# The gated product of the expert pairs on GpSimd, in two operations, in place of VectorE

## What is computed

```python
# top-4 of 32 experts per token; rows sorted by expert, cut into blocks
gu = xe @ w_gu[e] + b_gu[e]                       # 1024 -> 2048
gate = jnp.minimum(gu[..., 0::2], 7.0)
up = jnp.clip(gu[..., 1::2], -7.0, 7.0)
act = (up + 1.0) * (gate * jax.nn.sigmoid(gate * 1.702))
y = act @ w_dn[e] + b_dn[e]                       # 1024 -> 1024
out = zeros.at[row_tok].add(y * row_gate)
```

## Time and profile before

| | |
|---|---|
| median of 3 runs | 1425.97 us |
| profiled execution, own time | 1428.16 us |
| its span | 1426.5 us |
| PE matmul busy | 1331.1 us, 93% |
| PE weight load busy | 1058.9 us, 74% |
| VectorE (DVE) busy | 1276.3 us, 89% |
| ScalarE (ACT) busy | 1026.1 us, 72% |
| GpSimd (POOL) busy | 439.6 us, 31% |
| moved by DMA | 472.83 MB, mean 331 GB/s |
| splits on VectorE, L1004 | 409 of 2283 ns mean |
| copies on ScalarE, L645 | 409 of 1921 ns mean |

### The profile page before, as it was taken

The page is one execution under the profiler, slowest core; times in us unless marked ns, Lnnn a source line. Parts: engine busy times, 40 slices in busy tenths (PEclk is TensorE's granted clock), DMA queues, the critical chain, the costliest instruction groups (busy, mean ns, idle before and its releaser), DMA issues.

```text
span 1426.5 us, 20070 instructions
## 1 busy us (share of the span) xinstructions
PE 1331.1 (93%) x6410; PEld 1058.9 (74%) x6410; DVE 1276.3 (89%) x1246; ACT 1026.1 (72%) x945; POOL 439.6 (31%) x286
## 2 busy tenths in 40 slices
PE   6999989898999999999999999999999999999996
PEld 5876866776877777787877777777878777788883
DVE  7448665689999999999999999999999999999998
ACT  5344444447788888878788888888787888877772
POOL 0000000023143536253444435362535444311100
PEclk9999999999999999999999999999999999999998
DMA  9511130279999999999999999999999999999994
GB/s 352 192 59 60 35 133 31 83 264 382 378 395 403 402 393 406 409 403 405 406 406 400 402 394 404 397 401 406 403 398 400 408 397 396 390 380 374 364 372 178
DMA packets 85573, 472.83 MB, mean 331 GB/s; under 512 B 16619, under 2 KB 16659, under 8 KB 34336
## 3 DMA queue, kind: packets, MB, share of 16 engines
q1 hardware_dynamic: 70736, 451.79, 79.6%
q0 software_dynamic: 14800, 20.55, 4.1%
HBM read 467.80 MB, written 22.02 MB: 343 GB/s over the span
## 4 chain that ended last, share of the span: by engine, by line
PE 50%; DVE 22%; issue 13%; DMA 7%; ACT 6%; POOL 0%; DVEq 0%; SPq 0%; POOLq 0%; ACTq 0%
DVE w_lo L1004 11%; PE gu_bank L1536 10%; PE gu_bank L1538 9%; PE gu_bank L1537 9%; DMA raw<-in_w_down_dram 5%; ACT w_hi L645 4%; PE turn_bank L1536 3%; PE turn_bank L1537 3%; PE turn_bank L1538 3%; DVE arena L1384 2%; PE bank L1536 1%; PE bank L1538 1%; PE bank L1537 1%; PE bank L1861 1%; DVE arena L1394 1%
## 5 line engine op out<-in xcount | busy, mean ns | idle before, releaser
L1004 DVE TENSOR_TENSOR w_lo<-raw,w_hi 128x2048 fp32r<-128x2048 f32 x409 | 916.4, 2283 | 61.1 <-ACT w_hi L645 60.1
L645 ACT ACTIVATE w_hi<-raw 128x2048 fp32r<-128x2048 f32 x409 | 771.9, 1921 | 120.7 <-PE gu_bank L1538 96.2
L610 POOL DMA_INDIRECT expert_rows<-arena x32 | 215.9, 6747 | 303.7 <-ACT arena L831 147.7
L1536 PE MATMUL gu_bank<-w_hi,turned 128*128 128x512 f32 x624 | 246.6, 395 | 3.8 <-DVE w_lo L1004 3.7
L1538 PE MATMUL gu_bank<-w_hi,turned 128*128 128x512 f32 x624 | 243.3, 390 | 0.0
L1537 PE MATMUL gu_bank<-w_lo,turned 128*128 128x512 f32 x624 | 243.1, 390 | 0.0
L1542 PE MATMUL gu_bank<-w_hi,turned 128*128 128x512 f32 x448 | 180.0, 402 | 29.2 <-DVE w_lo L1004 27.9
L1543 PE MATMUL gu_bank<-w_lo,turned 128*128 128x512 f32 x448 | 175.1, 391 | 0.0
L1536 PEld LDWEIGHTS gu_bank<-w_hi,turned 128*128 128x128 f32 x624 | 117.2, 188 | 33.6 <-DVE w_lo L1004 6.6
L584 POOL COPY arena<-arena 128x1 int32 (+1 forms) x32 | 53.0, 1657 | 285.7 <-PE bank L1854 275.1
L1538 PEld LDWEIGHTS gu_bank<-w_hi,turned 128*128 128x128 f32 x624 | 117.1, 188 | 24.8
(11 more groups left out here) (343 smaller groups left out, 1786.4 us busy)
## 6 DMA issues: line engine op xcount, KB each, us to landing
raw<-in_w_gate_up_dram SPq DMA_DIRECT2D x264, 1024.0 KB, 9.5
raw<-in_w_down_dram SPq DMA_DIRECT2D x132, 1024.0 KB, 8.4
raw<-in_w_in_dram SPq DMA_DIRECT2D x10, 1024.0 KB, 7.2
raw<-in_w_out_dram SPq DMA_DIRECT2D x4, 1024.0 KB, 5.1
raw<-expert_rows SPq DMA_DIRECT2D x4, 1024.0 KB, 6.5
turned<-split_biases POOLq DMA_DIRECT2D x132, 4.0 KB, 6.7
raw<-in_w_mem_kv_dram SPq DMA_DIRECT2D x2, 1024.0 KB, 12.5
arena<-in_x_dram SPq DMA_DIRECT2D x1, 2048.0 KB, 13.9
```

Source lines behind the costliest of these rows:

```text
L610: pool.indirect_dma_start(y_dram, bass.IndirectOffsetOnAxis(idx_scatter, 0), y_row, None, bounds_check=TOPK * S - 1, oob_is_err=False).the ...
L645: a.activation(home, raw_ap, ACT.Copy).then_inc(hi_ready, halves)
L1004: v.tensor_tensor(home[1], raw_ap, home[0].bitcast(F32), ALU.subtract).then_inc(lo_ready, halves)
L1536: pe.matmul(bank, a[0], b[0], start=first, stop=False)
```

## The change

For the blocks 2 to 29 the product that `activate` made leaves VectorE's program. GpSimd makes it in its loop, after the bias rows and before the scatter, in two operations: the limit, in place in `sig_t`, and the product with `up_t`. Between the two it waits for its own semaphore. `clamp` gets a wait for `act_ready` of the block before, since `up_t` is read later than it was. GpSimd's loop is cut in two, one with the product and one, from block 30, without; there and in block 1 VectorE keeps it.

```diff
+            def gated(n):
+
+                pool.wait_ge(sig_ready, n)
+                pool.wait_ge(atp_done, n - 1)
+                pool.sem_inc(gated_go, 1)
+                pool.tensor_scalar(sig_t, sig_t, SIG_LIMIT, None, ALU.min).then_inc(sig_limited, 1)
+                pool.wait_ge(sig_limited, n - 1)
+                pool.tensor_tensor(act, sig_t, up_t, ALU.mult).then_inc(act_ready, 1)
+
+            def steps(first, end, low):
+
+                with pool.Fori(first, end) as b:
+                    pool.wait_ge(xtp_done, b + 1)
+                    gather(bass.ds(b + 1, 1), b * 2)
+                    bias_of_block(b)
+                    if low:
+                        gated(b)
+                    scatter(b - 2, b * 2 + 1)
+
+            steps(2, LOOP_FROM, True)
+            steps(LOOP_FROM, loops, False)
...
-            def clamp(n, folded=None):
+            def clamp(n, folded=None, used=None):
...
+                if used is not None:
+                    v.wait_ge(act_ready, used)
...
             # wide_after_narrow
-                clamp(b + 1)
+                clamp(b + 1, used=b)
...
-                activate(b + 1, b)
...
             # narrow_after_wide
-                clamp(b + 1, folded)
+                clamp(b + 1, folded, b)
                 lo_m(GU + 12, b)
-                activate(b + 1, b, NARROW_ROWS)
```

More of the change, by code:

```diff
@@ L320, in hymba_layer @@
         atp_done, ahi_ready, alo_ready = sem("atp_done"), sem("ahi_ready"), sem("alo_ready")
-        x_kept = sem("x_kept")
+        x_kept, sig_limited, gated_go = sem("x_kept"), sem("sig_limited"), sem("gated_go")
         ones_ready, bias_saved, bias_now_in = sem("ones_ready"), sem("bias_saved"), sem("bias_now_in")
```

## The result

The changed kernel takes 1469.49 us (median of 4 runs, 1466.99 to 1470.43) against 1426.16 us for the one before (now four runs): a ratio of 1.0303, 95% interval 1.0285 to 1.0321. It is slower by 43 us. The forecast had the sign right and the size three times too large (133 us); the rival called "turn about" had said 1474.

A forecast was written before the change was run, and what follows sets the result against it. VectorE and the weight transfers were taken to bound the kernel together. Losses of 1.8 + 7.7 = 9.5 us a pair over 14 pairs, 133 us, gave 1559 us, range 1442 to 1622.

The forecast's parts named there:

- turn about: Rival: GpSimd enters at the next split's border, holding the split behind for the product's length; 3.4 us a pair, 1474; chance 0.25.
- Two resources at their limit, transfers 0.4 us above VectorE: Two-block pairs of the expert loop: VectorE and transfers both limit; in later pairs transfers bind, some 0.4 us above VectorE's pace.
- The removal gives 0.45 and 0.35 us: Taking the gated products off VectorE gains 0.45 (even body) and 0.35 us (odd), until ScalarE's copy binds; 0.8 a pair.
- Even body, 1.8 us: Wide-after-narrow block: GpSimd's product enters late and holds VectorE's remaining split 2.2 us; less 0.45 gained, 1.8 us lost.
- a hair's gap: Even body: the tiny gap before the sixth split, at about 727.75, where the product was to enter, ending at 730.
- Odd body, 7.7 us: Narrow-after-wide block: the product waits out six splits, runs 765.3 to 767.6; TensorE's transposes start 7.7 us late, all lost.
- Prices on GpSimd: Assumed for GpSimd's new operations: product 2.2 us (1.1 to 4.4), limit 1.1 (0.6 to 2.2), wait behind own operation 0.89.
- the 5.04 us of one small copy: GpSimd's index copy at 414.77 sat out three splits; taken as evidence that GpSimd reads wait while splits run back to back.
- Chances: First case 0.33, no gap in the even body 0.22, turn about 0.25, covered same 0.10, covered faster 0.07, worse 0.03.

The follow-up runs named there:

- the second run: Kernel before, plus a GpSimd product of 1024 columns on unused rows at the change's place, nothing waiting for it: 1484.23 us, ratio 1.0406.
- the third run: Kernel before, plus a one-input GpSimd limit operation of 1024 columns on an unused row at the change's place: 1442.66 us, ratio 1.0111.
- the eleventh: Changed kernel without the limit operation, GpSimd's product also waiting until VectorE ended the second split behind the sigmoid: 1454.25 us, ratio 1.0188.
- the fifth run: Kernel before, plus a spare GpSimd product at the head of GpSimd's pass, right before the index copy: 1452.57 us, ratio 1.0178.
- The first run: Changed kernel without limit and product for blocks 2 to 29, semaphore waits kept, TensorE transposing old rows: 1429.46 us, ratio 1.0017.
- the seventh: Changed kernel without limit and product, waits kept, every expert weight transfer cut to half its columns: 1417.32 us, ratio 0.9933.
- sixth: Kernel before with every expert weight transfer cut to half its columns, all engine instructions kept: 1420.07 us, ratio 0.9954.

## Why the prediction was wrong

- *Two resources at their limit, transfers 0.4 us above VectorE.* Right: with half the bytes the pair is 65.00 in place of 65.34.
- *The removal gives 0.45 and 0.35 us.* Right in VectorE's stretches (0.39 and 0.36), wrong as a gain: TensorE's wide part took 0.25 of it back, granted-clock dips more, and with full transfers nothing was left (ratio 1.0017).
- *Even body, 1.8 us.* Measured 1.75. The sum was right, its path was not, so the match is partly luck: the product entered at the first border at 735.9, not in a hair's gap ten microseconds later, and between 400 and 1240 us no wait of TensorE for the activation shows. A held split costs the same wherever VectorE sets the pace.
- *Odd body, 7.7 us.* This is the step that failed. I let the product wait for six splits, until 765.3, and TensorE for the product, since index copies had sat out up to three splits. It entered at the first border, about 2.3 us after the split of 701.87 began. The stretch grew by 1.92 us and the wide part gave 0.52 back: 1.40 in place of 7.7. That is 6.3 us in 14 pairs, 88 us, and the forecast was off by 90. Being shut out until the turn is something that a product can meet (one of 26 in the second run); that it meets it every time was the error.
- *Prices on GpSimd.* The product at 2.2 us was right as what it holds the port for (2.21). The limit at 1.1 was too low in its row (2.82 alone) and too high in its hold (0.84). The wait behind the own operation was 0.08 us (735.11 to 735.19) and not 0.89. Limit and wait together were 2.90 us where I had 2.0; so the errors offset only in part.
- *Turn about.* The rival had the mechanism: first border, one split held for the product's length. It gave 3.4 us a pair and 1474; measured 2.86 and 1469.5. The Trainium skill (SBUF — State Buffer, "Who interferes with whom") has it that a VectorE instruction with two SBUF inputs contends with a GpSimd one that reads SBUF, and that the ports the two share are an exclusive lock; of VectorE's two-port modes it says that whoever issues first has them for the whole instruction while the other fully blocks. The trace agrees on the block: 4.50 us in place of 2.29. It differs on the length: the limit operation's row is 2.8 to 3.5 us long in the third run and held VectorE for 0.84 at most. I had set the rule aside for the 5.04 us of one small copy, and a copy that took 14.39 us across six splits is indeed not what one lock per instruction would give.
- *Chances.* 0.25 on the case that came, 0.55 on cases some 90 us and more away. Rows of an operation of another size, 128x1, had outweighed a rule and a row that both spoke for the nearer case.

What stays open: why a GpSimd operation sits out several splits in some places and enters at the first border in others. Small copies do both, and so do large operations. The product that was shut out in the second run came 0.5 us behind the start of a split; those of the eleventh, which all entered at its end, came 0.35 us behind one. In the changed kernel the scatter, whose indices also lie in the arena, has rows of 1.8 to 2.2 us in the pairs, in the kernel before of 6.7 to 9.0 but for one; and in the fifth run the products missed a border 0.6 us ahead of them, but not the next. Neither the arrival time nor how far ScalarE's copy is ahead of the split sorts the cases in these traces.

The first run says that nothing is to be won this way: with the product gone altogether the time at the full transfers is 1.0017 of the one before.

## What to carry to other kernels

Before work is moved to GpSimd, list what VectorE runs beside it: here an instruction with two inputs in SBUF was held for most of a GpSimd product's time, so a product of 1.14 us removed from VectorE came back as 2.2 us of standing still. If it must be done, put it under instructions that read PSUM, or into a gap: the same product cost 22 us less when it came 2.9 us sooner, without the limit ahead of it. Take the product out altogether first, to see what relief is worth; here that run, at 1.0017, would have said beforehand that there was nothing to win.

## What the runs showed of the hardware

- A GpSimd operation's row is longer than the time for which it holds VectorE: 2.8 to 3.5 us against 0.84 for the one-input form on 1024 columns (third run), 2.6 against 2.2 for the product (changed kernel, odd body).
- The hold strikes whatever VectorE instruction with two SBUF inputs comes next, a split or the gated product (1.21 to 3.43 us), and is in proportion to the columns (1.1 us for 512). Turns and clamps, with an input in PSUM, kept their 0.4 to 1.2 us in the pairs of all traces, beside GpSimd's operations too.
- GpSimd's scatters shrank from a median of 6.78 us to 1.98 without any change to them, and in the first run, with no product at all, to 1.8 to 2.0 in the pairs. So most of their long rows before was waiting, not work; that it was for the read of the indices is my guess.
- An operation of GpSimd can be shut out while VectorE runs splits back to back: a copy for 14.39 us, a product for 15.07, a limit for 15.42, each until VectorE's next turn. It is rare for the large ones (2 of some 350 products and limits in the pairs of ten traces).
- The granted clock has dips that the kernel before does not show between 380 and 1240 us: a mean of 0.91 over 20 us, which is some 3.4 us at the lower of its two levels (1.2 GHz, against 2.4). In that stretch the changed kernel's trace has three, from 398, 467 and 535 us on, the first run's six, the second's fifteen, the seventh's three, those of the third, fifth and sixth none. A pair with one is about 1.4 us longer (65.87 against 64.50) in the seventh run; in the changed kernel VectorE's first stretch is 23.56 us with or without one. What brings them was not tested.
